# A dense layer whose gate and up products are kept transposed, with the weights stationary and 512 tokens moving

## The reference, cut to what matters

```python
D_MODEL, D_FF = 1024, 2816
def _swiglu(h, w_gu, w_down):
    gu = h @ w_gu                       # (512, 1024) @ (1024, 5632)
    f = w_gu.shape[-1] // 2
    return (jax.nn.silu(gu[..., :f]) * gu[..., f:]) @ w_down
```

## Time and profile before

| | us |
|---|---|
| median of 3 runs | 2213.79 |
| lowest and highest | 2212.46, 2215.01 |
| the profiled execution, its own time | 2220.81 |
| its span, first to last instruction | 2218.7 |

### The profile page before, as it was taken

One profiled execution on the slowest core, in us unless ns is written; L12 is line 12 of the kernel. 1 busy time (PEld: TensorE's weight loads), 2 busy tenths in 40 slices (PEclk: granted clock), 3 DMA queues, 4 the chain that ended last, 5 costly groups with the idle time before them and its releaser, 6 DMA issues. The chain is left out here.

```text
span 2218.7 us, 34004 instructions
## 1 busy us (share of the span) xinstructions
PE 2028.2 (91%) x12819; PEld 1732.7 (78%) x12820; DVE 1562.3 (70%) x1882; ACT 1314.4 (59%) x1752; POOL 94.6 (4%) x81
## 2 busy tenths in 40 slices
PE   3989979999999688988786999999999999999997
PEld 3967879998998576776585888878888888878885
DVE  2155345456554667767755989898998989898997
ACT  4135364446444345355445877878777777878775
POOL 0000000000000012322400000000000000000000
PEclk8999989999999799999797999999999999999998
DMA  8359724554553121121062999999999999999994
GB/s 309 115 195 383 259 69 160 182 179 152 188 174 118 47 88 58 57 77 39 1 210 95 374 344 362 345 354 343 365 363 337 361 336 364 347 347 342 372 358 157
DMA packets 272544, 517.19 MB, mean 233 GB/s; under 512 B 10459, under 2 KB 97835, under 8 KB 272427
## 3 DMA queue, kind: packets, MB, share of 16 engines
q1 hardware_dynamic: 272427, 515.57, 65.3%
HBM read 514.49 MB, written 1.05 MB: 232 GB/s over the span
## 5 line engine op out<-in xcount | busy, mean ns | idle before, releaser
L1788 DVE TENSOR_TENSOR lo<-raw,hi 128x1024 fp32r<-128x1024 f32 x880 | 1066.1, 1231 | 370.3 <-ACT hi L1299 282.2
L1316 ACT ACTIVATE hi<-raw 128x1024 fp32r<-128x1024 f32 x672 | 710.5, 1063 | 197.1 <-PE bank L690 197.1
L688 PE MATMUL bank<-hi,xh_t 128*128 128x256 f32 (+1 forms) x2016 | 676.0, 335 | 28.6 <-DVE lo L1788 11.6
L689 PE MATMUL bank<-lo,xh_t 128*128 128x256 f32 (+1 forms) x2016 | 670.8, 333 | 0.0
L690 PE MATMUL bank<-hi,xl_t 128*128 128x256 f32 (+1 forms) x2016 | 670.8, 333 | 0.0
L688 PEld LDWEIGHTS bank<-hi,xh_t 128*128 128x128 f32 x2016 | 388.3, 193 | 69.8 <-issue 23.0
L689 PEld LDWEIGHTS bank<-lo,xh_t 128*128 128x128 f32 x2016 | 388.4, 193 | 37.2 <-issue 1.9
L690 PEld LDWEIGHTS bank<-hi,xl_t 128*128 128x128 f32 x2016 | 388.1, 193 | 35.4
L1299 ACT ACTIVATE hi<-raw 128x1024 fp32r<-128x1024 f32 x208 | 218.4, 1063 | 298.6 <-PE bank L690 279.9
L688 PE MATMUL bank<-hi,hth 128*128 128x512 f32 x624 | 252.3, 404 | 0.8 <-DVE lo L1788 0.2
L690 PE MATMUL bank<-hi,htl 128*128 128x512 f32 x624 | 243.6, 390 | 0.0
(11 more groups left out here) (271 smaller groups left out, 1790.3 us busy)
## 6 DMA issues: line engine op xcount, KB each, us to landing
raw<-in_moe_gu_w_dram SPq DMA_DIRECT2D x224, 1024.0 KB, 6.8
raw<-in_moe_down_w_dram SPq DMA_DIRECT2D x112, 1024.0 KB, 6.1
raw<-in_ada_w_dram SPq DMA_DIRECT2D x24, 2048.0 KB, 9.8
raw<-in_ffn_gu_w_dram SPq DMA_DIRECT2D x44, 1024.0 KB, 5.1
raw<-in_ffn_down_w_dram SPq DMA_DIRECT2D x22, 1024.0 KB, 4.9
raw<-in_ssm_in_w_dram SPq DMA_DIRECT2D x16, 1024.0 KB, 5.3
raw<-in_ssm_out_w_dram SPq DMA_DIRECT2D x8, 1024.0 KB, 5.6
raw<-in_mix_in_w_dram SPq DMA_DIRECT2D x5, 1024.0 KB, 12.5
```

The source lines that it names most:

```text
L688: mm(o, a_hi, w_hi, start=first, stop=False, **kw)
L689: mm(o, a_hi, w_lo, start=False, stop=False, **kw)
L1316: A_(hi[:, p % SPL, :], raw[:, u, (p % 2) * PIECE:(p % 2 + 1) * PIECE], ACT.Copy).then_inc(m_hi, 1)
L1788: TT(lo[:, p % SPL, :], raw[:, u, h * PIECE:(h + 1) * PIECE], hi[:, p % SPL, :].bitcast(F32), ALU.subtract).then_inc(done, 1)
```

## The change

Gate and up are computed once, for all 512 tokens, with the weights stationary: a 128-column block of `hi` or `lo` is loaded, and 512 columns of `xh` or `xl` move. The result is already transposed (hidden width on partitions), so the transposes go. Eight banks are used in two sets of four by step parity. The products h, 22 chunks of 128 x 512, stay in SBUF: 16 in raw slots 2 to 5, 6 in a free part of `ar`. In step 0 the latent half of the tokens is taken first and the context half behind norms 6 and 7. Down then runs over all 22 chunks for the latent tokens, and again for the context: in each pass and chunk two blocks and two halves of the columns, three matmuls each, 12 of 512 columns for each piece of w_down. A chunk's 256 tokens are split just before (`h_hi`, `h_lo`), four chunks ahead, into what were `hth` and `htl`. w_gu is loaded once (22 units), w_down in each pass (11 and 11). While the layer runs, the ring has two raw slots. Posts and norms 8 and 9 move into the second down pass; n counts its pieces from 0. The semaphore offsets of the expert stage follow. In the diff, a line of three dots stands for lines left out; the removed functions are those printed above.

```diff
@@ -49,6 +49,8 @@
 FFN_STEPS = D_FF // UCOL
+FFN_CHUNKS = 2 * FFN_STEPS
+FFN_SLOTS = 2
 MCOL = 512
...
@@ -240,11 +231,17 @@
         grow = [m5.take(D_MODEL) for _ in range(4)]
-        sg = [m5.take(UCOL) for _ in range(2)]
-        hb = [m5.take(UCOL) for _ in range(2)]
+        sg = [m5.take(512) for _ in range(2)]
         ptmp = m5.take(D_MODEL)
...
+        h_rest = ar[:, m4.at - 2 * D_MODEL:m4.at + D_MODEL]
+        fth, ftl = (t[:, :, :].rearrange("p a (c n) -> p (a c) n", c=2) for t in (hth, htl))
+        def hcol(q):
+            return raw[:, FFN_SLOTS + q // 4, (q % 4) * 512:(q % 4 + 1) * 512] if q < 16 else \
+                h_rest[:, (q - 16) * 512:(q - 15) * 512]
         s0 = Arena(0)
@@ -364,9 +362,11 @@
         def slot(u):
-            first_u, end_u = unit_of_split(S_DT), unit_of_split(S_SSMOUT)
+            ffn_u, first_u, end_u = (unit_of_split(s) for s in (S_FFN, S_DT, S_SSMOUT))
+            if u < ffn_u:
+                return u % RAW
             if u < first_u:
-                return u % RAW
+                return (u - ffn_u) % FFN_SLOTS
             return (u - first_u) % (RAW // 2) if u < end_u else (u - end_u) % RAW
...
@@ -475,9 +474,18 @@
         P_MOE = 2 * S_MOE
-        FFN_N = len(order_ffn)
+        P_UP, P_DOWN = 2 * S_FFN, 2 * S_FFN + 4 * FFN_STEPS
         J_SLOTS, J_GATHER = 3, 5
-        C_MOE, T_MOE, Y_MOE = 2 * 2 * FFN_STEPS, 2 * FFN_STEPS, 8
+        C_MOE, Y_MOE = FFN_CHUNKS, 8
+        def wait_from(eng, s, n):
+            if not isinstance(n, int) or n > 0:
+                eng.wait_ge(s, n)
+        def ffn_bank(j, i):
+            return bank[4 * ((j + 1) % 2) + i]
         block = es.enter_context(nc.Block())
@@ -535,15 +543,13 @@
             gu, dn = A["ffn_gu_w"][0], A["ffn_down_w"][0]
-            for ps in range(2):
...
+            for j in range(FFN_STEPS):
+                for i in range(2):
+                    load_cols(S_FFN + 2 * j + i, gu, j * UCOL + i * D_FF)
+            for i in range(2 * FFN_STEPS):
+                s = S_FFN + 2 * FFN_STEPS + i
+                u, r = unit_of_split(s), i % FFN_STEPS * UCOL
+                load(u, "split", s, rawv(u, 2), dn[r:r + UCOL, :].rearrange("(t p) n -> p t n", p=P))
             w_in = A["ssm_in_w"][0]
...
@@ -552,6 +558,8 @@
                 sp.dma_start(rawv(u, 8)[:, :, P:2 * P], wcols(w_in, c0 + g * P, P)).then_inc(raw_landed[slot(u)], 16)
+                if g == 0:
+                    sp.wait_ge(f_lo, FFN_CHUNKS + 4)
                 for i in range(2):
...
@@ -870,74 +878,60 @@
             pe.wait_ge(grow_ready, 2)
-            def swiglu(s0, nblk, n, pos, xoff, c0, t0, y_free, at_step=None):
...
+            pe.wait_ge(xsplit_done, 6)
+            def up(j, kind, n0, n1):
+                for h in range(2):
+                    p = P_UP + 4 * j + 2 * kind + h
+                    pe.wait_ge(lo_ready, p + 1)
+                    if h == 0 and j >= 2:
+                        pe.wait_ge(h_done if kind else sil_done, 2 * j - 2)
+                    for c in range(2):
+                        o = ffn_bank(j, 2 * kind + c)[:, n0:n1]
+                        for t in range(4):
+                            k = 4 * h + t
+                            w_hi, w_lo = wpart(p, t, UCOL, c * P, P)
+                            mm(o, w_hi, xh[:, k, n0:n1], start=(k == 0), stop=False)
+                            mm(o, w_hi, xl[:, k, n0:n1], start=False, stop=False)
+                            m = mm(o, w_lo, xh[:, k, n0:n1], start=False, stop=(k == KC - 1))
+                    if n1 == 4 * P:
+                        m.then_inc(piece_used, 1)
+            def down(q):
+                ps, i = divmod(q, FFN_CHUNKS)
+                p = P_DOWN + q
+                pe.wait_ge(lo_ready, p + 1)
+                pe.wait_ge(f_lo, q + 1)
+                if i == 0:
+                    pe.wait_ge(h_done, FFN_CHUNKS - 2 + 2 * ps)
+                for b in range(2):
+                    for half in range(2):
+                        m = tok3(bank[4 * ps + 2 * b + half][:, :], fth[:, q % 4, b * P:(b + 1) * P],
+                                 ftl[:, q % 4, b * P:(b + 1) * P], *wpart(p, 0, 1024, half * 512, 512),
+                                 first=(i == 0), last=(i == FFN_CHUNKS - 1))
+                m.then_inc(piece_used, 1)
+            up(0, 0, 0, 2 * P)
+            norm_t(6)
+            norm_t(7)
+            up(0, 1, 0, 2 * P)
+            pe.wait_ge(xsplit_done, 8)
+            up(0, 0, 2 * P, 4 * P)
+            grow_(2)
+            grow_(3)
+            up(0, 1, 2 * P, 4 * P)
+            pe.wait_ge(grow_ready, 4)
+            for j in range(1, FFN_STEPS):
+                up(j, 0, 0, 4 * P)
+                up(j, 1, 0, 4 * P)
+            for q in range(2 * FFN_CHUNKS):
+                if q == FFN_CHUNKS + 7:
+                    pe.wait_ge(y_evac, 4)
+                if q in (FFN_CHUNKS + 7, FFN_CHUNKS + 8):
+                    norm_t(q - FFN_CHUNKS + 1)
+                down(q)
             pe.wait_ge(y_evac, 8)
...
@@ -1475,54 +1469,54 @@
             norm_a(7)
-            def swiglu(s0, nblk, n, pos, c0, t0, sgt, look, at_step=None):
...
+            def h_hi(q):
+                act.wait_ge(h_done, q % FFN_CHUNKS + 1)
+                if q >= 4:
+                    act.wait_ge(piece_used, P_DOWN + q - 3)
+                n0 = q // FFN_CHUNKS * 2 * P
+                A_(fth[:, q % 4, :], hcol(q % FFN_CHUNKS)[:, n0:n0 + 2 * P], ACT.Copy).then_inc(f_hi, 1)
+            def y_out(ps):
+                act.wait_ge(piece_used, P_DOWN + (ps + 1) * FFN_CHUNKS)
+                for half in range(2):
+                    A_(y[:, 2 * ps, half * 512:(half + 1) * 512], bank[4 * ps + half][:, :], ACT.Copy).then_inc(y_evac, 1)
+            norm_b(6)
+            norm_b(7)
+            for j in range(FFN_STEPS):
+                p = P_UP + 4 * j
+                hi_to(p + 1 + SPL)
+                hi_to(p + 2 + SPL)
+                act.wait_ge(piece_used, p + 2)
+                for c in range(2):
+                    if j >= 1:
+                        act.wait_ge(h_done, 2 * j - 1 + c)
+                    A_(sg[c], ffn_bank(j, c)[:, :], ACT.Silu).then_inc(sil_done, 1)
+                if j == 0:
                     grow_out(2)
...
-                if j == 0 and ps == 1:
+                hi_to(p + 3 + SPL)
+                hi_to(p + 4 + SPL)
+                if j == FFN_STEPS - 3:
+                    for q in range(4):
+                        h_hi(q)
+            for q in range(2 * FFN_CHUNKS):
+                hi_to(P_DOWN + q + 1 + SPL)
+                if q + 4 < 2 * FFN_CHUNKS:
+                    h_hi(q + 4)
+                n = q - FFN_CHUNKS
+                if n == -1:
+                    y_out(0)
+                if n in (1, 2):
                     act.wait_ge(y_evac, 4)
-                    post_a(4)
...
+                    post_a(n + 3)
+                if n in (4, 5):
+                    norm_a(n + 4)
+                if n in (9, 10):
+                    norm_b(n - 1)
+            y_out(1)
             act.wait_ge(y_evac, 8)
...
@@ -1983,48 +1977,48 @@
             norm_a(7)
-            def swiglu(s0, nblk, n, pos, c0, t0, sgt, ht, look, at_step=None):
...
+            def h_lo(q):
+                dve.wait_ge(f_hi, q + 1)
+                n0 = q // FFN_CHUNKS * 2 * P
+                TT(ftl[:, q % 4, :], hcol(q % FFN_CHUNKS)[:, n0:n0 + 2 * P], fth[:, q % 4, :].bitcast(F32), ALU.subtract
+                   ).then_inc(f_lo, 1)
+            def y_out(ps):
+                dve.wait_ge(piece_used, P_DOWN + (ps + 1) * FFN_CHUNKS)
                 for half in range(2):
-                    dve.tensor_copy(y[:, 2 * ps + 1, half * 512:(half + 1) * 512], bank[2 + half][:, :]).then_inc(y_evac, 1)
+                    dve.tensor_copy(y[:, 2 * ps + 1, half * 512:(half + 1) * 512], bank[4 * ps + 2 + half][:, :]
+                                    ).then_inc(y_evac, 1)
+            norm_b(6)
+            norm_b(7)
+            for j in range(FFN_STEPS):
+                p = P_UP + 4 * j
+                for i in range(3):
+                    lo_to(p + i + 1 + SPL)
+                dve.wait_ge(piece_used, p + 4)
+                for c in range(2):
+                    dve.wait_ge(sil_done, 2 * j + c + 1)
+                    TT(hcol(2 * j + c), sg[c], ffn_bank(j, 2 + c)[:, :], ALU.mult).then_inc(h_done, 1)
+                lo_to(p + 4 + SPL)
+                if j == FFN_STEPS - 3:
+                    for q in range(4):
+                        h_lo(q)
+            for q in range(2 * FFN_CHUNKS):
+                lo_to(P_DOWN + q + 1 + SPL)
+                if q + 4 < 2 * FFN_CHUNKS:
+                    h_lo(q + 4)
+                n = q - FFN_CHUNKS
+                if n == -1:
+                    y_out(0)
+                if n in (2, 3):
+                    post(n + 2)
+                if n in (5, 6):
+                    norm_a(n + 3)
+                if n in (10, 11):
```

(33 more changed lines are left out.)

146 lines of the change are left out of this document (8 added, 138 removed).

## The result

| | before | after |
|---|---|---|
| median of 4 runs each | 2214.40 us (2212.46 to 2221.28) | 2193.42 us (2192.17 to 2196.09) |
| ratio | | 0.9902, 95% interval 0.9888 to 0.9916 |
| profiled execution, its span | 2220.81 us, 2218.7 us | 2193.92 us, 2192.1 us |
| dense layer, first gate matmul to last down matmul and one pitch (the distance from one start to the next) | 401.0 us | 377.0 us |
| from there to the first 512-column matmul of the SSM projection | 29.1 us | 27.1 us |

The kernel became faster by 21.0 us, with the interval by 18.6 to 24.8 us. The two traces differ by more, 26.6 us of span: 24.0 of it in the layer, 2.0 behind it (742.86-713.77 against 717.45-690.40), 1.2 in the rest, less 0.6 by which the layer starts later.

What follows compares the result with a forecast made beforehand. The dense layer was taken as bound by TensorE's own stream; -12.8 -10.1 -5.5 -0.9 +7.0 = -22.3 us, off the median 2213.79, gave 2191.5 us, range 2183 to 2200.

Steps and rivals of the forecast that it cites:

- wait for norm 8: Second down pass: TensorE stands some 4.1 us before norm 8's transposes because VectorE's queue is late.
- the clock behind it: After the idle time before norm 8's transposes, about 5.9 us at half speed cost 2.9 us more.
- Gate and up (-12.8): Gate and up: 960 pairs of 256-column matmuls become single 512-column ones, 0.2267 instead of 0.240 us each, 12.8 us less.
- The rival built on halves that cost what a whole does: Gate and up: a 512-column matmul costs its two halves' 0.240 us, so no gain per matmul; 2204.3 us, chance 0.07.
- Transposes (-10.1): Dense layer: the 22 transpose groups go, at 0.46 us each with the slow start behind them, 10.1 us less.
- The seam (-5.5): Between the old passes: 2.98 us of idle time and 27 matmuls at the lower clock go, 5.5 us less.
- The start: Layer start: cold start and gate broadcasts stay; TensorE waits 1.2 us for the context tokens' split.
- Splits and loads hidden: Dense layer: 44 fewer splits on each engine and 22 MB less to load, all hidden, nothing gained.
- Norms 8 and 9 (+7.0): Second down pass: late norms make TensorE wait and drop its clock, 7.0 us more, bounds 0 and 8.7.
- The rival without a wait: Second down pass: VectorE gets through its queue in time, the 7.0 us fall away; 2184.5 us, chance 0.22.
- The raw slots (0): Down's loads: going from 6 raw slots to 2 costs 0, bounds 0 and 6 us.
- the rival's arithmetic: Down: w_down loads through two slots set the pace; 2197.5 us at 7.6 us to landing, 2236.5 at 12.1; chance 0.12.

Runs made afterwards that it cites:

- e3: Changed kernel with up's steps 1 to 10 moving 256 tokens at a time instead of 512: 2205.13 us, ratio to before 0.9950.
- e5: Changed kernel with 20 groups of four transposes put back in the first down pass, into an unread bank: 2200.85 us, ratio to before 0.9934.
- e4: Changed kernel with one more TensorE wait between up and down, for the first four w_down pieces to be split: 2192.51 us, ratio to before 0.9895.
- e11: Changed kernel with up's splits done twice and one SiLU put before the evacuation at the layer's end: 2193.52 us, ratio to before 0.9909.
- e1: Changed kernel with norms 8 and 9 two pieces later in the second down pass: 2186.56 us, ratio to before 0.9867.
- e8: Changed kernel with one small 32 KB load issued and awaited before each load of w_down: 2193.93 us, ratio to before 0.9910.
- e9: Changed kernel with two small 32 KB loads in series before each load of w_down: 2219.95 us, ratio to before 1.0018.
- e12: Changed kernel with only the TensorE transposes of norms 8 and 9 one piece earlier: 2201.55 us, ratio to before 0.9948.
- e0: The changed kernel measured again without any edit: 2193.11 us, ratio to before 0.9906.
- e2: Changed kernel with norms 8 and 9 one piece later in the second down pass: 2186.06 us, ratio to before 0.9864.

## Why the prediction came true

**The size.** Predicted 22.3 us less, measured 21.0; 2191.5 against 2193.42. The layer was to take 378.7 us and took 377.0. Part by part (the two rows of matmuls are a count times the pitch in the trace):

| | predicted us | measured us |
|---|---|---|
| start, to the first 512-column matmul | 32.3 | 32.4 |
| 960 matmuls of up | 217.6 | 217.6 |
| 528 of down | 119.7 | 119.7 |
| wait for norm 8 | 4.1 | 3.7 |
| the clock behind it | 2.9 | 1.7 to 1.8 |
| transposes of norms 8 and 9 | 2.1 | 1.8 |

**Gate and up (-12.8)**: right, by the pitch in after and by e3. The Trainium skill's formula in TensorE: Matmul & The Clock Gate, section Back-to-back issue gap (N/2.4 + 2.5 ns at the full clock, 216 ns for 512 columns), is given there for an isolated matmul, and it doesn't hold for this stream: 226.7 ns in after, and 0.120 us for 256 columns in e3, as before. The rival built on halves that cost what a whole does fell.

**Transposes (-10.1)**: right, e5 puts 0.47 us on a group.

**The seam (-5.5)**: no idle time is left there. What it was worth stands on one execution of before, and no median shows it. It doesn't split as I had it into an idle time and a clock that always follows: e4 has the idle time and not the clock.

**The start**: the chain of modulation, cast and subtraction gave 1.2 us of wait, measured 1.16. **Splits and loads hidden**: right, by e11 for the splits.

**Norms 8 and 9 (+7.0)**: the mechanism was right and the wait nearly so. On VectorE's timeline of after, with the end of piece 2 of the second pass at 563.46+25*2.72 = 631.5 us, post 4 starts, then norm 8's scaling:

```profile
635.42 0.16 DVE L1849 RECIPROCAL rstd<-rms 128x1 f32<-128x1 f32 x1
...
645.33 0.75 DVE L1835 TENSOR_SCALAR ar<-xres,rstd 128x1024 f32<-128x1024 f32 x1
```

That is 3.9 us and, at its end, 14.6 us after that moment, where I had 4.2 and 14.9. Piece 6 ends 10.9 us after that moment and not 10.7, so the sum should have said 4.0; from start to start the wait is 3.85 us, and 3.69 as the trace counts idle time. The rival without a wait, to which I gave 0.22, is what e1 made true by moving two steps of the order; its price, 2184.5, was near e1's 2186.56. The term that was mis-sized is the clock: "about 5.9 us at half speed as in the earlier trace rows cost **2.9 us** more". That was the stretch at the old start, halved, where the matmuls of the same rows give 27*0.093 = 2.5. Behind norm 8 it was 3.5 us, from 647.0 to 650.5, and cost 1.7 to 1.8: what e1's layer gained (5.5) beyond the wait (3.7), and what e3's fell short of 12.8.

**The raw slots (0)**: right, and the rival's arithmetic fits once the lead of the buffers, 9 us, is taken off. It was to decide "from some 9.5 us to landing"; e8, at 1.7+4.9 = 6.6, cost nothing, and e9, at 10.1, lost 23.2 us of layer and ended slower than before by 0.18% (0.08 to 0.28%). The prediction took off the lead at 12.1 us and not elsewhere: at 9.5 us the formula gives 25-9 = 16 us and not 25, and it eats the gain of 22.3 only from 10.0; at 7.6 us I gave a bound of 6 us lost, where it gives none. No run stood between 6.6 and 10.1, so where the loss begins is not shown. "In time by a hair" was too dark: 1.7 us later is still in time.

**A term that wasn't in the sum.** Before, the root of post 6 stood behind a table load of 1.28 us, because a SiLU had run since the last root. In the new order the posts and norms 8 and 9 take their roots after the last SiLU (a table load at 631.37 us, the last in the layer), and nothing but copies, squares and the modulation of the norms follows, so the table is still there. That gives 1.27 us at the root (6.2 against 4.93 us behind the layer's end) of the 2.0 us gained behind the layer. The other 0.8 is the clock. The second 24 matmuls of the small DT projection stood behind an idle time of 6.07 us in before and 6.31 in after. TensorE's timelines of before, then of after, their first and the next stage:

```profile
736.36 0.47 PE L688 MATMUL bank<-xh_t,hi 128*64 128x256 f32 x1 [6.07 <-DVE xl_t L1848]
...
742.47 0.46 PE L960 MATMUL bank<-con,ar 64*128 64x64 f32 x4 [0.73 <-ACT ar L1537]
```

```profile
711.73 0.47 PE L696 MATMUL bank<-xh_t,hi 128*64 128x256 f32 x1 [6.31 <-DVE xl_t L1842]
...
715.36 0.28 PE L698 MATMUL bank<-xh_t,lo 128*64 128x256 f32 x1
...
717.05 0.46 PE L954 MATMUL bank<-con,ar 64*128 64x64 f32 x4 [0.74 <-ACT ar L1531]
```

That is 6.11 and 5.32 us. In after the last seven run at the full clock, in before all 24 at the lower one. In the variants of the changed kernel the same stretch takes 5.1 us (e1) to 6.1 (e3), and 6.03 in e11, so these 0.8 us can't be put down to the change.

**What stays open.** The traces give 24.0 us for the layer and 1.3 for the table load, the medians 21.0 (18.6 to 24.8) for everything. The changed layer repeats to 0.1 us in four traces (377.0, 377.0, 376.9, 376.9), but there is one trace of before, an execution 6.4 us above its median. Some of the 24.0 may be that execution's own; outside the layer and the stretch behind it, it took 1788.6 us, and the thirteen traces of the changed kernel and its variants 1782.9 to 1789.5. The medians by themselves give 11.7 us to the wider matmuls (e3) and 8.5 to the transposes (e5), 20.2 of the 21.0. What is left for the seam, the edges, the wait before norm 8 and the root together is 0.8 us, where the traces give 2.8. So the two main terms are shown either way; that 22.3 came so near to 21.0 is in part luck, as the two traces by themselves give 26.0.

## What to carry to other kernels

Where one engine's stream bounds a stage, count its instructions and its idle stretches first, each with a duration from a row: in this layer fewer and wider matmuls gave 13 ns each, dropped transposes 0.47 us a group, and halving the splits nothing. When steps of side work are moved into a denser stage, walk each in-order queue in time up to the moment the bound engine wants the result, and place the request one or two pieces later than that; a request too early cost its wait and the clock behind it (after), and in e12 a second wait through the buffers that TensorE didn't free. For a ring of load slots, work out the period of the loop that each wait closes (landing, splits, release) against the consumer's period: here a delay of 1.7 us was free, one of 5.2 us took 23, and nothing between was tried.

## What the runs showed of the hardware

The granted clock did not follow the length of the idle time alone. Behind the wait of 3.67 to 3.69 us before norm 8 it fell to the 1.2 GHz level in six profiles (after, e0, e4, e5, e8, e11) and not in e3; it fell behind 2.83 us in before, and didn't behind 2.51 us in e4, nor behind the second wait of e12, 3.66 us. So an idle time of such a length has to be priced with and without its clock, 1.7 us apart behind norm 8. Nor did it always fall at once. Before the first matmuls of the DT projection TensorE idled for 3.60 us in e1, e2 and e3 and 3.61 in after, and the pitch of 256 columns went from 0.12 to 0.21 us at once in e1 and e3, behind four matmuls in after and behind some ten in e2.

The small loads of 32 KB landed in 1.7 us (median) one at a time; two in series ahead of a unit took 3.35 us from the free slot to its issue where the unit before had landed, and 5.2 us in the case shown, beside one.
